# A hybrid decoder in fp32 on one core: a longer ring of expert weights, one buffer for silu and its product, and TensorE's full-array products gathered in five places per pair of experts

## The reference, cut to what matters

```python
def swiglu(u, w_gate_up, w_down):
    g, up = jnp.split(u @ w_gate_up, 2, axis=-1)
    return (jax.nn.silu(g) * up) @ w_down

for ex in range(N_EXPERTS):          # 8 experts, D_MODEL 1024, E_FF 3584
    y = y + gate[:, ex:ex + 1].astype(tok.dtype) * swiglu(tok, w_gate_up[ex], w_down[ex])
```

## Time and profile before

| | |
|---|---|
| median of 3 runs | 1364.03 us (1361.99 to 1365.8) |
| the profiled execution, device time | 1364.19 us |
| its span in the trace | 1361.6 us |
| TensorE busy | 1302.9 us, 96% of the span |
| moved by DMA | 423.81 MB |
| chain that ended last | PE 75%, DMA 9%, DVE 6%, SP's queue 6% |

### The profile page before, as it was taken

How to read it: one execution, slowest core, us unless ns; L and a number is a source line. 1 busy time by engine, 2 the same in 40 slices (tenths; PEclk the granted TensorE clock), 3 DMA queues, 4 the chain that set the end, 5 groups by cost and what they waited for, 6 DMA issues and landing times.

```text
span 1361.6 us, 26236 instructions
## 1 busy us (share of the span) xinstructions
PE 1302.9 (96%) x11384; PEld 744.6 (55%) x11384; DVE 421.7 (31%) x804; ACT 348.7 (26%) x659; POOL 54.4 (4%) x81
## 2 busy tenths in 40 slices
PE   8989999999889899999999999989999989999986
PEld 7988999999788773343333443332343332333322
DVE  7785766643688541001110001000000100000102
ACT  7885544443577630000000000000000000000001
POOL 3001100001220120000000000000000000000000
PEclk9999999999999979999999999999999999999999
DMA  9537455555132469999999999999999999999994
GB/s 291 165 100 254 141 184 171 180 165 172 52 129 76 143 245 338 369 379 373 414 418 417 416 417 418 415 418 418 415 418 419 415 417 419 415 417 419 416 417 187
DMA packets 127955, 423.81 MB, mean 311 GB/s; under 512 B 8272, under 2 KB 77136, under 8 KB 99168
## 3 DMA queue, kind: packets, MB, share of 16 engines
q1 hardware_dynamic: 127664, 421.58, 79.9%
q0 software_dynamic: 176, 0.53, 0.1%
HBM read 421.03 MB, written 1.05 MB: 310 GB/s over the span
## 4 chain that ended last, share of the span: by engine, by line
PE 75%; DMA 9%; DVE 6%; SPq 6%; ACT 3%; issue 1%; DVEq 0%
PE bank L874 29%; PE bank L855 13%; PE bank L484 8%; PE bank L486 8%; PE bank L485 8%; SPq L1004 6%; DMA ring<-in_m_w_down 5%; DMA ring<-in_m_w_gate_up 4%; PE bank L832 1%; PE bank L813 1%; DVE w_lo L1505 1%; PE bank L845 1%; PE bank L847 1%; DVE rstd L1525 1%; ACT w_hi L1123 1%
## 5 line engine op out<-in xcount | busy, mean ns | idle before, releaser
L874 PE MATMUL bank<-ring,x_T 128*32 128x512 f32 (+1 forms) x5120 | 491.0, 540 | 7.4 <-DMA ring<-in_m_w_gate_up 6.0
L874 PEld LDWEIGHTS bank<-ring,x_T 128*32 128x32 f32 x5120 | 162.3, 110 | 322.3 <-issue 295.7
L855 PE MATMUL bank<-ring,eT 128*32 128x512 f32 x2240 | 249.7, 594 | 14.1 <-DMA ring<-in_m_w_down 14.1
L484 PE MATMUL bank<-u_hi,w_hi 128*128 128x272 f32 (+2 forms) x632 | 184.5, 292 | 6.9 <-DVE u_lo L1560 5.1
L486 PE MATMUL bank<-u_hi,w_lo 128*128 128x272 f32 (+2 forms) x632 | 182.2, 288 | 0.0
L485 PE MATMUL bank<-u_lo,w_hi 128*128 128x272 f32 (+2 forms) x632 | 181.6, 287 | 0.0
L1505 DVE TENSOR_TENSOR w_lo<-raw,w_hi 128x2048 fp32r<-128x2048 f32 (+7 forms) x89 | 143.9, 1639 | 94.6 <-ACT w_hi L1123 94.4
L855 PEld LDWEIGHTS bank<-ring,eT 128*32 128x32 f32 x2240 | 68.4, 110 | 180.0 <-issue 145.8
L1123 ACT CAST w_hi<-raw 128x2048 fp32r<-128x2048 f32 (+7 forms) x89 | 117.9, 1352 | 52.9 <-PE bank L486 52.9
L484 PEld LDWEIGHTS bank<-u_hi,w_hi 128*128 128x128 f32 (+1 forms) x632 | 118.7, 188 | 11.1 <-issue 5.0
L485 PEld LDWEIGHTS bank<-u_lo,w_hi 128*128 128x128 f32 (+1 forms) x632 | 118.8, 188 | 0.0
(11 more groups left out here) (302 smaller groups left out, 1231.9 us busy)
## 6 DMA issues: line engine op xcount, KB each, us to landing
ring<-in_m_w_gate_up SPq DMA_DIRECT2D x128, 1024.0 KB, 23.3
ring<-in_m_w_down SPq DMA_DIRECT2D x112, 1024.0 KB, 24.2
ring<-in_m_w_gate_up SPq DMA_DIRECT2D x128, 768.0 KB, 21.4
raw<-in_f_w_gate_up SPq DMA_DIRECT2D x24, 1024.0 KB, 5.3
raw<-in_f_w_down SPq DMA_DIRECT2D x12, 1024.0 KB, 5.3
raw<-in_a_w_in SPq DMA_DIRECT2D x10, 1024.0 KB, 8.5
raw<-in_a_w_out SPq DMA_DIRECT2D x8, 640.0 KB, 4.7
raw<-in_b_w_o SPq DMA_DIRECT2D x4, 1024.0 KB, 5.2
```

Source lines behind the costliest of these rows:

```text
L484: nc.tensor.matmul(o, a[0], b[0], start=start, stop=False)
L855: return nc.tensor.matmul(strip(q, t, NT), eT[u][:, bank, P * i + GROUP * at:P * i + GROUP * at + GROUP], w[:, n, :], start=start, stop=stop)
L874: last = nc.tensor.matmul(strip(q + 3 * (kind_of == "up"), t, width), x_T[:, part, group(g)], w[:, width * n:width * n + width], start=(pa ...
```

## The change

Four things change in the expert loop, and nothing ahead of it but the places of buffers in SBUF:

- the ring has 17 units instead of 14, and since 84 isn't a multiple of 17, places are given for a whole pair (`OFFSETS`, 85 units with what is skipped at the end of a lap); `used_before` works over the pair
- `e_silu` is gone: ScalarE writes silu into `e_h`, and VectorE multiplies in place
- TensorE's full products stand together: in BIG all turns of section 0 after piece 17, and the turns of section 1, `gather_x` and `turn_gated` after piece 33; in SMALL the whole scatter after piece 3, the turns of section 0 after piece 17, and the rest after piece 33
- these products use other banks (`TURNED_IN`, `BACK`), the waits follow them, and VectorE's copy to `selT` stands after it has taken the next tokens. The semaphore `selT_zeroed` is merged into `selT_done`.

```diff
+TURNED_IN = ((6, 7, 5), (0, 1, 2))
+
+BACK = ((2, 5), (6, 7))
...
-RING = 14 * CHUNK
+RING = 17 * CHUNK
...
-OFFSET = [sum(WORDS[:c]) % RING for c in range(EC)]
+def ring_offsets():
+
+    offsets, at = [], 0
+    for n in WORDS + WORDS:
+        if at % RING + n > RING:
+            at += RING - at % RING
+        offsets.append(at % RING)
+        at += n
+    assert at % RING == 0
+    return offsets
...
-        e_silu = sb("e_silu", [P, NGS[BIG], NT])
...
                     if u == 0 and q == 0:
                         pe.wait_ge(y_left, ex + 1)
                         pe.wait_ge(y_right, ex * 3 + 3)
-                        pe.wait_ge(selT_done, ex + 1)
-                    if u == 0 and q == 2:
-                        pe.wait_ge(eT_by_act, it * EA_PAIR + EA_BEFORE[kind] + 1)
+                        if kind == SMALL:
+                            pe.wait_ge(scatter_added, it * 4 + 8)
...
+                        if c == UP_END[0] - 7 and kind == BIG:
+                            pe.wait_ge(selT_done, ex + 2)
+                        if c == UP_END[1] - 7 and kind == BIG:
+                            pe.wait_ge(eT_by_act, it * EA_PAIR + EA_BEFORE[kind] + ng - 1)
...
+                    if c == 3 and kind == SMALL:
+                        scatter()
                     if c == GATE_END[1] - 6:
-                        turn(0, 0)
-                        turn(0, 1)
-                    if c == GATE_END[1] - 4 and kind == BIG:
-                        turn(0, 2)
+                        for q in range(ng):
+                            turn(0, q)
                     if c == DOWN + 1:
                         for q in range(ng):
                             turn(1, q)
-                    if c == DOWN + 6:
                         for half in range(2):
                             gather_x(half)
-                    if c in (1, 6) and kind == SMALL:
-                        scatter(c // 6)
-                    if c == 11:
                         turn_gated()
...
                     at_expert(act, it, kind, "chunk", GATE_END[u])
-                    act.wait_ge(eh_done, it * EH_PAIR + EH_BEFORE[kind] + ng * u)
                     for q in range(ng):
-                        nc.scalar.activation(e_silu[:, q, 0:width], banks[q][:, 0:width], ACT.Silu).then_inc(silu_done, 1)
+                        nc.scalar.activation(e_h[:, q, 0:width], banks[q][:, 0:width], ACT.Silu).then_inc(silu_done, 1)
```

More of the change, by code:

```diff
@@ L127, with used_before @@
 DOWN = 4 * KD
[L128 to L136, removed]
+assert EC % 2 == 0
+def used_before(kind, c):
+    p = EC * kind + c
+    for d in range(p + 2 * EC - 1, -1, -1):
+        o, n = OFFSETS[d % (2 * EC)], WORDS[d % EC]
+        if o < OFFSETS[p] + WORDS[c] and OFFSETS[p] < o + n:
+            return d - 2 * EC
 TURNED = ((), (0, 1, 2), (3, 4, 5), (6, 7))
@@ L791, in landed_chunk @@
                     pe.wait_ge(ring_landed[c % LANDINGS], ex * 32 + 16 * (c // LANDINGS + 1))
-                    return ring[:, OFFSET[c]:OFFSET[c] + WORDS[c]]
+                    at = OFFSETS[EC * kind + c]
+                    return ring[:, at:at + WORDS[c]]
                 def strip(q, t, width):
@@ L817, in turn_gated @@
                 def turn_gated():
-                    pe.wait_ge(y_left, ex + 1)
-                    pe.wait_ge(y_right, ex * 3 + 3)
                     pe.wait_ge(gated_done, ex + 1)
+                    if kind == SMALL:
+                        pe.wait_ge(scatter_added, it * 4 + 8)
                     for b in range(NB):
-                        last = nc.tensor.transpose(banks[7][0:CAP, P * b:P * b + P], gated_sel[:, b, :], ident)
+                        last = nc.tensor.transpose(banks[5][0:CAP, P * b:P * b + P], gated_sel[:, b, :], ident)
                     emark(last, ("gated",))
@@ L834, in gather_x, with scatter @@
                     emark(last, ("x", half))
-                def scatter(n):
+                def scatter():
                     pe.wait_ge(y_left, ex + 1)
                     pe.wait_ge(y_right, ex * 3 + 3)
[L840 to L849, removed]
+                    pe.wait_ge(selT_done, ex + 2)
+                    for n in range(2):
+                        for b in range(NB):
+                            ps = banks[BACK[n][b]]
+                            nc.tensor.matmul(ps[:, :], selT[BIG][0:CAP, b, :], y_big[0:CAP, NT * n:NT * n + NT],
+                                             start=True, stop=False)
+                            last = nc.tensor.matmul(ps[:, :], selT[SMALL][0:CAP, b, :], y_small[0:CAP, NT * n:NT * n + NT],
+                                                    start=False, stop=True)
+                            emark(last, ("scattered", NB * n + b))
                 def weigh(q, t, block, g, n, w, start, stop):
@@ L916, in _ @@
             last_ex = rounds * NE
-            pe.wait_ge(selT_done, last_ex)
+            pe.wait_ge(selT_done, last_ex + 2)
             for n in range(2):
@@ L1103, in _ @@
                 nc.gpsimd.memset(y_small[:, c], 0.0).then_inc(*((y_left, 1), (y_right, 3))[part])
-            nc.gpsimd.memset(selT[BIG][:], 0.0).then_inc(selT_zeroed, 1)
-            nc.gpsimd.memset(selT[SMALL][:], 0.0).then_inc(selT_zeroed, 1)
+            nc.gpsimd.memset(selT[BIG][:], 0.0).then_inc(selT_done, 1)
+            nc.gpsimd.memset(selT[SMALL][:], 0.0).then_inc(selT_done, 1)
             nc.gpsimd.memset(acc[:], 0.0).then_inc(scatter_added, 4)
@@ L1417, in _ @@
                     i = 2 * b + half
-                    nc.scalar.activation((e_silu, e_h)[b][:, half, :], banks[i][:, :], ACT.Square, accum_out=halves[:, i:i + 1])\
+                    nc.scalar.activation((eT[0], e_h)[b][:, half, :], banks[i][:, :], ACT.Square, accum_out=halves[:, i:i + 1])\
                         .then_inc(h_summed, 1)
```

37 lines of the change are left out of this document (18 added, 19 removed).

## The result

| | before | after |
|---|---|---|
| median of 5 runs, first comparison | 1365.80 us | 1356.00 us |
| ratio, 95% interval | | 0.9937 (0.9922 to 0.9953) |
| the same kernels again, ratio | | 0.9951 (0.9932 to 0.9970) |
| a third time, ratio | | 0.9932 (0.9919 to 0.9945) |
| profiled execution, device time | 1364.19 us | 1354.27 us |

The change makes the kernel faster, by 0.5 to 0.7% in the three comparisons. The forecast was 1358 us, 0.45% faster; 1353 to 1362.5 us was the range.

What follows compares the result with a forecast made beforehand. The bound was the transfers from the queue's last dry moment on: the issue at piece 22 comes 6.4 us earlier with the same 273.5 units left, so 1364.19 us becomes 1357.8, called 1358 us; range 1353 to 1362.5 us.

Steps and rivals of the forecast that it cites:

- The bound: Whole kernel: the end is the last moment the transfer queue runs dry, plus bytes left over the rate, 413 GB/s.
- Where it runs dry last: First SMALL: SyncE pauses at the same piece 22, now held up by piece 4 instead of piece 7.
- One sign named for it: After SyncE's pause ending at 641 to 642 us, issue-to-landing was to stay over 10 us.
- When TensorE gets there: First SMALL: TensorE through piece 4 at 641.2 us, issue at 641.6 instead of 648.0; 0.3 us saved a visit.
- The bytes left: From piece 22 of the first SMALL on: the same 273.5 units, 698.7 us at 2.55 us a unit.
- The bounds: Limits on the gain: 8.5 us if transfers don't run dry behind the scatter, 2.8 if the joined scatter loses 3.6.
- One buffer: Section 1's silu needs e_h free; the transposes reading it stand six pieces or 11 us earlier, so no cost.
- the early turn: BIG's turn 2 moves from piece 19 to 17; its wait for VectorE's third product is covered by 1.8 us.
- the scatter's wait: The scatter needs y_big, done at 629.2 us; it moves from 629.9 to 632.4, margin from 0.7 to 3 us.
- No change: Rival, chance 0.19: gain 4 us or less, from the joined scatter or a later dry moment in the second SMALL; 1360 to 1363.
- Slower: Rival, chance 0.06: the deeper ring lowers the transfer rate over the last 700 us, 7.0 us each 1%; 1368 us at 1.5%.
- It goes further: Rival, chance 0.12: transfers don't run dry at piece 22 and earlier dry moments are bridged too; down to about 1352 us.

Runs made afterwards that it cites:

- order alone: The changed kernel with the ring back at 14 units and e_silu kept for the squares ahead of the loop: 1363.45 us, ratio 0.9996 to the kernel before.
- ring alone: The kernel before with the ring of 17 units, OFFSETS and the single buffer, TensorE's products where they stood: 1355.38 us, ratio 0.9936.
- the first five experiments: Ring alone 0.9936, order alone 0.9996, the scatter after piece 9 0.9921, the gather back at piece 38 0.9932, the late pieces 14 to 16 0.9936.
- the scatter after piece 9: The changed kernel with the whole scatter of SMALL after piece 9 instead of piece 3: 1353.77 us, ratio 0.9921; timed again 1354.35 us, 0.9917.
- the late pieces 14 to 16: The changed kernel with pieces 14 to 16 of the first lap held back until TensorE has done pieces 0 to 2: 1357.20 us, ratio 0.9936.
- extra products: Added to the kernel with the scatter after piece 9: an unused 128-column identity product after each of eight router-logit steps; 1360.17 us, ratio 0.9949.
- the gather back at piece 38: The kernel with the scatter after piece 9, with gather and gated transposes also moved from after piece 33 to 38: 1355.36 us, ratio 0.9932.

## Why the prediction was right, point by point

**The bound.** The transfers, from the last dry moment to the end. Right: with TensorE's work cut the time stayed (order alone, 0.9996), and a change of 3 units in the ring moved it (ring alone, 0.9936). But "ran dry" and "hardly two pieces in flight" were too strong. 7.6 us to land at 2.55 us a unit are three units, and when piece 22 was issued 1.5 units were still under way before the change, 0.75 after it. The sum leaves this difference out. And "room is no matter" after 700 us isn't so: in the trace before, SyncE waits 69 times for TensorE to free room there, 122.7 us in all, up to 6.0 us at a time. It costs nothing because 17 us and more of transfers are under way (with the ring of 17 it is 24 times and 42.2 us). The 28 us for which TensorE was said to stand still are 20.1 us of waits in the rows.

**Where it runs dry last.** Right: piece 22 of the first SMALL, held up by piece 4. 131.4 us after the loop's start were worked out, 131.35 measured. One sign named for it came only in part: issue-to-landing was to stay over 10 us afterwards; it is 6.9 us at 642 and over 10 for good from 645.5 us on.

**When TensorE gets there.** SMALL was to start 115.2 us into the loop (625.4 - 510.2) and did at 115.18; the scatter to run from 122.2 to 129.3 us and ran from 122.16 to 129.22. The three visits saved 0.96 us, 0.32 each, where 0.3 was taken.

**The bytes left.** 273.5 units in 698.7 us were carried over, and it took 698.27. Gain by the sum 6.4 us, by the loop 6.8 to 7.2. From the low point of the queue to the last piece a unit takes between 2.552 and 2.560 us in seven profiles (both kernels and the first five experiments), wherever the low point lies; that is what the rule rests on.

**The bounds.** The loss from joining the scatter's halves, put at 3.6 us at most, turned out to be nearly nothing net: the ring alone has the same loop to 0.1 us. Joining them moves the pause from piece 26 to piece 22, which is 6.4 us earlier with 3 units more left (7.6 us), and with the 0.96 us of the visits in it the two nearly cancel. The prediction's sum came out right, but it didn't say this: all of its 6.4 us could have been had from the ring, and none from TensorE's order.

**One buffer, the early turn, the scatter's wait.** No cost, as said: TensorE has no wait for VectorE or ScalarE in the loop apart from its start. VectorE's third product ended 1.8 us ahead of the transposes, as in the kernel before:

```profile
548.77 1.89 DVE L2001 TENSOR_TENSOR e_h<-bank,e_h 128x512 f32<-128x512 f32 x3 [34.21 <-PE bank L894]
```

548.77 + 1.89 = 550.66, and the transposes start at 552.51.

**The rivals.** "No change" rested on a pause in the second SMALL that would cost something; there was none, since from 700 us on nothing lands in under 17 us. "Slower" rested on a lower rate with a deeper ring; it is 413 GB/s in both, though SyncE's issues became longer. "It goes further" didn't come by itself, but two of its microseconds were there to be had by moving the scatter.

**What wasn't foreseen** is the loop's start, which the prediction took as 510.2. It moved by -2.9 us in the first profile; without that, this execution would have taken 1357.2 us. That the median fell 2 us below the forecast, to 1356.0, is in part luck of this kind. The start varies without any change: one and the same kernel (the scatter after piece 9) started its loop at 507.20 us in one profile and at 510.26 in the other. How much of it may still belong to the change, the spans of all runs bound. I take the loop before as 836.6 us, the mean of its two profiles. Between the medians of a comparison the span falls by 7.75 and 8.3 us for the changed kernel, 0.7 and 1.4 more than the loop does, and by 0.6 and 0.8 more for the ring alone and the late pieces 14 to 16; but for the three timings with the scatter after piece 9 and no extra products (one of them with the gather back at piece 38) it falls by 0.1 to 1.5 us less than the loop. What lies outside the loop has no steady sign and stays within 1.5 us. The loop alone gives a ratio of 0.995; two of the three intervals hold that, the third ends at 0.9945.

## What to carry to other kernels

Where transfers and compute are nearly as fast as each other, don't ask which is busier, but when the transfer queue is last nearly empty: issue-to-landing times show it, and from there the end is bytes over rate, here to within 1 or 2 us. Buffer depth counted at that moment (6.9 us for 3 units), and the same depth at the start of the loop counted for nothing. Work saved on the compute engine behind that moment only makes it wait longer; that work saved ahead of it counts in full follows from the rule, but no run here shows it by itself, since the 0.96 us saved went together with the joined scatter. A block of work that frees no room is best put where more is under way: 2.1 us for the scatter moved by six pieces, and nothing more for the gather.

## What the runs showed of the hardware

- SyncE's issue of a piece takes 0.33 us when few are in flight, and a median of 1.5 us, up to 7, when many are the earlier trace rows; after the change it is 1.9 us for gate and up and 1.5 for down, up to 8.3. With three more units of room, the time from issue to landing hardly rose after 700 us: 23.8 us before, and after the change

```profile
DMA to landing us min/median/max: 18.5/24.8/30.6
```

  So some ten units are in flight, at 2.5 us each, with either ring. With the ring of 17 SyncE waits less for room (42.2 us after 700 us for 122.7) and longer in its issues, so more room hardly brought more into flight. That the queue itself has this limit is my reading of it; no run here changed it.
- Going from products with 32 columns to full ones and back costs 0.3 us a visit (0.32 measured over three). That agrees with the Trainium skill, page "TensorEngine Tiling (Array Packing)", § Tiling Modes, which says that a change of mode drains the array.
- The stretch ahead of the loop, where TensorE has many short products and waits, is granted 1.2 GHz for 7 to 17 us, differently from one execution to the next, and that moves the start of the loop by up to 3 us. The kernel with the scatter after piece 9 in its two profiles (the third number from the right is the granted clock, 1.00 for 2.4 GHz); the first starts its loop at 507.20 us, the second at 510.26:

```profile
490.00:512.00 22.00, 18.76 (x129) 12.60 (x131) 14.64 (x73) 10.29 (x24) 4.18 (x7) 0.84 0.70 268
```

```profile
490.00:512.00 22.00, 20.43 (x99) 16.36 (x100) 12.31 (x62) 10.29 (x24) 4.17 (x7) 0.61 0.67 268
```

  The other kernels without extra products fit in, with either ring: at 0.84 in this window the loop starts at 507.0 to 508.0 us, at 0.77 at 508.5 and 508.95, at 0.69 at 510.3 and at 0.61 at 510.2 to 511.6. The 32 products of the first gather took 7.11 us in the profile of the kernel before (0.61) and 3.78 in the first one of the changed kernel (0.84).
